# Front half of a hybrid decoder layer: four x tiles and one subtraction for each form, V in four banks, sums read from PSUM, stores spread

## What is computed

```python
h = rms_norm(x, norm_g[l])
proj = jnp.einsum('bsd,de->bse', h, w_in[l])
u_pool, z_pool, q, k, v, z_attn, gate_logits = jnp.split(proj, splits, axis=-1)
y_pool = multiscale_pool(u_pool, pool_w[l], pool_scale[l]) * jax.nn.silu(z_pool)
attn = stick_breaking_attention(q, k, v)
...
x = x + jnp.einsum('bsd,de->bse', merged, w_out[l])
return rms_norm(x, final_g)
```

## Time and profile before

| | |
|---|---|
| median of 3 runs | 1658.92 us (1653.3 to 1668.74) |
| profiled execution | 1660.69 us, of which the span 1658.9 us |
| mean granted clock of TensorE | 0.979 |
| busy PE / DVE / ACT / POOL | 94% / 82% / 50% / 72% of the span |
| front half | up to 439 us of the span |

### The profile page before, as it was taken

The page is one execution under the profiler, slowest core; times in us unless marked ns, Lnnn a source line. Parts: engine busy times, 40 slices in busy tenths (PEclk is TensorE's granted clock), DMA queues, the critical chain, the costliest instruction groups (busy, mean ns, idle before and its releaser), DMA issues. The chain is left out here.

```text
span 1658.9 us, 25189 instructions
## 1 busy us (share of the span) xinstructions
PE 1552.7 (94%) x7770; PEld 1285.2 (77%) x7770; DVE 1354.2 (82%) x1753; ACT 824.9 (50%) x1597; POOL 1188.5 (72%) x818
## 2 busy tenths in 40 slices
PE   7897888988899999899998999999999999999998
PEld 5686666867678788788787788888888878877886
DVE  6987499795699788899789988889988765587988
ACT  4433443332456666566566566666666622133342
POOL 4695585875698877988788788779997534446774
PEclk9998999999999999999999999999999999999999
DMA  6376961247423434334279333343522578764453
GB/s 229 122 276 205 331 196 58 71 121 195 148 84 93 112 100 122 97 100 133 74 231 345 94 106 104 98 119 88 153 78 55 181 241 274 243 219 166 154 190 126
DMA packets 170277, 254.20 MB, mean 153 GB/s; under 512 B 48401, under 2 KB 81681, under 8 KB 170146
## 3 DMA queue, kind: packets, MB, share of 16 engines
q1 hardware_dynamic: 170146, 252.59, 49.5%
HBM read 166.54 MB, written 85.99 MB: 152 GB/s over the span
## 5 line engine op out<-in xcount | busy, mean ns | idle before, releaser
L1828 DVE TENSOR_TENSOR_SCAN left<-keep,left 128x512 f32<-128x512 f32 x192 | 301.3, 1569 | 38.0 <-issue 29.0
L1901 POOL TENSOR_TENSOR ring<-raw,ring 128x512 fp32r<-128x512 f32 x140 | 236.7, 1690 | 80.9 <-ACT ring L1735 65.7
L1655 PE MATMUL psum<-hT,ring 128*128 128x512 f32 x664 | 273.3, 412 | 12.2 <-ACT sum_a L1767 7.0
L1659 PE MATMUL psum<-hT,ring 128*128 128x512 f32 x664 | 271.2, 408 | 0.0
L1657 PE MATMUL psum<-hT,ring 128*128 128x512 f32 x664 | 270.8, 408 | 0.0
L1741 ACT ACTIVATE keep<-psum 128x512 f32<-128x512 f32 (+3 forms) x320 | 171.2, 535 | 128.4 <-PE psum L1678 112.0
L1748 ACT ACTIVATE wt<-psum 128x512 fp32r<-128x512 f32 (+3 forms) x320 | 171.2, 535 | 104.8 <-PE psum L1686 102.1
L1834 DVE TENSOR_TENSOR wt<-psum,wt 128x512 fp32r<-128x512 f32 (+3 forms) x320 | 189.5, 592 | 12.4 <-ACT wt L1748 9.5
L1698 PEld LDWEIGHTS psum<-wt,vm 128*128 128x128 f32 x1088 | 171.4, 189 | 33.9 <-DVE wt L1834 4.3
L1698 PE MATMUL psum<-wt,vm 128*128 128x256 f32 x1088 | 181.8, 282 | 6.4 <-DVE wt L1834 3.5
L1686 PE MATMUL psum<-ident,left 128*128 128x128 f32 x1088 | 171.3, 272 | 11.3 <-DVE wt L1834 11.1
(11 more groups left out here) (240 smaller groups left out, 3597.1 us busy)
## 6 DMA issues: line engine op xcount, KB each, us to landing
raw<-in_w_strips SPq DMA_DIRECT2D x144, 256.0 KB, 4.2
qm<-qk_scratch SPq DMA_DIRECT2D x128, 128.0 KB, 4.2
gate<-gate_scratch SPq DMA_DIRECT2D x64, 256.0 KB, 4.9
form_scratch<-hT SPq DMA_DIRECT2D x28, 512.0 KB, 7.0
hT<-form_scratch SPq DMA_DIRECT2D x28, 512.0 KB, 7.7
xT<-in_x_T SPq DMA_DIRECT2D x16, 512.0 KB, 4.9
qk_scratch<-front_store SPq DMA_DIRECT2D x32, 256.0 KB, 4.3
km<-qk_scratch SPq DMA_DIRECT2D x64, 128.0 KB, 3.8
```

The lines of the kernel that those rows point to most:

```text
L1655: pe.matmul(o, hi, m_hi, start=k == 0, stop=False)
L1659: last = pe.matmul(o, lo, m_hi, start=False, stop=k == HK - 1)
L1828: dve.tensor_tensor_scan(left[:, n % LN, span][:, ::-1], k, k, carry, ALU.mult, ALU.bypass).then_inc(scanned, 1)
L1901: pool.tensor_tensor(out_, a, b, op).then_inc(s, 1)
```

## The change

1. **Forms from x.** T1 to T4 are made from the scaled fp32 tiles, one subtraction each (four for a pair). For that four x tiles are resident; the fourth, `xT_last`, lies in the tile `store`. The load of xT of tile n now waits for T4 of the pair of tile n-4. DVE makes the low of T1 (and T2 of a phase's last pair), POOL the others (before, DVE made three of four, then two of four).
2. **Statistics two tiles ahead**, in the first tile phase: `square`, `mean`, `root`, `factors` of tile n+2 in the step of tile n; the diag is made by ACT. The step of tile 8 comes a slot earlier.
3. **V** has four PSUM banks (two are those of parts 2 and 3), the third product (low with high) of a tile is made in the slot of the next one, `copy_v` three tiles behind, with two staging buffers in turn for V and the mixes.
4. **Sums.** S1 is read from PSUM by DVE, ACT takes A11 only; seven adds per group, no joins. Three output tiles: A12 and A22 share one, S4 has one, S3 has one that lies in `b12`.
5. **Weight forms** S3 and S2 are made by DVE, S1 and S4 stay on POOL.
6. **Stores** of the forms go out three in four slots rather than one in each; V's pieces for stage 3 are asked for after parts 27, 31, 35, 39 rather than 29, 31, 33, 35.

```diff
-ADD_OF = {A12: 1, S2: 2, S3: 3, S4: 4, A22: 5}
+FRONT_ADD = {A12: 1, S2: 2, S1: 3, S3: 4, S4: 6, A22: 7}
+OUT_TILE = {A12: 0, S4: 1, S3: 2, A22: 0}
+OUT_AT = {A12: 1, S3: 5, S4: 6, A22: 7}
+BANK_READ = {A12: 1, S2: 2, S1: 5, S3: 4, S4: 6, A22: 7}
...
+    outs = (out_a, out_b, at("out_c", b12_at, [P, CH], F32)[:, :])
...
+    xT_last = at("xT_last", store_at, [P, KT, P], F32)
...
+    def x_tile(n):
+        return xT[:, n % 4, :, :] if n % 4 < 3 else xT_last[:, :, :]
...
-    V_PARTS = [HALF_PARTS + i for i in (29, 31, 33, 35)]
+    V_PARTS = [HALF_PARTS + i for i in (27, 31, 35, 39)]
...
+    STEP_AT = {n - 1: n for n in range(2, FRONT_TILES)}
+    STEP_AT.update({tile_slot(n) - (2 if n == FRONT_TILES else 1): n for n in range(FRONT_TILES, TT)})
...
-                elif n % FRONT_TILES >= 3:
-                    sp.wait_ge(lo_done, 2 * (n - 2))
-                    if (n - 3) % 2 == 1:
-                        sp.wait_ge(t_raw, RAW_OPS * ((n - 3) // 2) + RAW_OF[T2])
-                sp.dma_start(xT[:, n % 3, :, :], x_T[token_tile(n)]).then_inc(xT_in[n % 3], DMA)
+                    sp.wait_ge(t_raw, 4 * HK)
+                elif n % FRONT_TILES >= 4:
+                    sp.wait_ge(lo_done, 2 * (n - 3))
+                    sp.wait_ge(t_raw, 4 * ((n - 4) // 2 + 1))
+                elif n == FRONT_TILES + 3:
+                    for i in range(2):
+                        sp.wait_ge(hi_stored[i], 4 * qk_before(HALF_GROUPS) // 2 * DMA)
+                sp.dma_start(x_tile(n), x_T[token_tile(n)]).then_inc(xT_in[n % 4], DMA)
...
                 if n is not None:
-                    if n % FRONT_TILES >= 2:
-                        store_v(n - 2)
-                    if n % FRONT_TILES + 3 < FRONT_TILES:
+                    if n % FRONT_TILES >= 4:
+                        store_v(n - 4)
+                    if n % FRONT_TILES + 3 < FRONT_TILES and n != FRONT_TILES:
                         load_xT(n + 3)
                     if n < FRONT_TILES and n + 4 < FRONT_TILES:
...
+                if n == FRONT_TILES + 1:
+                    load_xT(n + 2)
...
-                    if r < len(FORM_LIST):
-                        store_form(*FORM_LIST[r])
+                    for i, form in enumerate(FORM_LIST):
+                        if i * 4 // 3 == r:
+                            store_form(*form)
...
-            def first_forms(n):
-                pair = n // 2
-                if n % FRONT_TILES == 1:
-                    for j in (T2, T1, T3):
+            def first_forms(pair):
+                n = 2 * pair + 1
+                if pair % HK == 0:
+                    for j in (T1, T2):
                         free_home(dve, n, j)
                 dve.wait_ge(scaled_done, 2 * n + 2)
-                dve.wait_ge(lo_done, 2 * n - 1)
+                dve.tensor_tensor(raw_t(n, T1), scaled(n, 0), scaled(n - 1, 0), ALU.subtract).then_inc(t_raw, 1)
+                dve.wait_ge(t_raw, 4 * pair + 1)
+                dve.tensor_tensor(raw_t(n, T2), scaled(n, 1), raw_t(n, T1), ALU.subtract).then_inc(t_raw, 1)
+
+            def last_forms(pair):
+                n = 2 * pair + 1
+                if pair % HK == 0:
+                    for j in (T3, T4):
+                        free_home(dve, n, j)
+                dve.wait_ge(t_raw, 4 * pair + 2)
                 dve.tensor_tensor(raw_t(n, T3), scaled(n, 1), scaled(n, 0), ALU.subtract).then_inc(t_raw, 1)
-                dve.tensor_tensor(raw_t(n, T1), scaled(n, 0), tile_of(n - 1, 0, 0).bitcast(F32),
-                                  ALU.subtract).then_inc(t_raw, 1)
-                dve.wait_ge(t_raw, RAW_OPS * pair + 2)
-                dve.tensor_tensor(raw_t(n, T1), raw_t(n, T1), tile_of(n - 1, 0, 1).bitcast(F32),
-                                  ALU.subtract).then_inc(t_raw, 1)
-                dve.wait_ge(t_raw, RAW_OPS * pair + RAW_OF[T1])
-                dve.tensor_tensor(raw_t(n, T2), scaled(n, 1), raw_t(n, T1), ALU.subtract).then_inc(t_raw, 1)
-
-            def last_form(n):
-                pair = n // 2
-                if n % FRONT_TILES == 1:
-                    free_home(dve, n, T4)
-                dve.wait_ge(t_raw, RAW_OPS * pair + RAW_OF[T2])
-                dve.wait_ge(lo_done, 2 * n)
-                dve.tensor_tensor(raw_t(n, T4), tile_of(n - 1, 1, 0).bitcast(F32), raw_t(n, T2),
-                                  ALU.subtract).then_inc(t_raw, 1)
-                dve.wait_ge(t_raw, RAW_OPS * pair + 5)
-                dve.tensor_tensor(raw_t(n, T4), raw_t(n, T4), tile_of(n - 1, 1, 1).bitcast(F32),
-                                  ALU.add).then_inc(t_raw, 1)
-
...
+                dve.tensor_tensor(raw_t(n, T4), scaled(n - 1, 1), raw_t(n, T2), ALU.subtract).then_inc(t_raw, 1)
+
+            def form_low(pair, j):
+                n = 2 * pair + 1
+                dve.wait_ge(t_hi, 4 * pair + RAW_OF[j])
+                dve.tensor_tensor(low_t(n, j), raw_t(n, j), high_t(n, j).bitcast(F32), ALU.subtract).then_inc(t_lo_dve, 1)
 
             def tile_step(n):
                 i = n % FRONT_TILES
-                first = n < FRONT_TILES
-                if first and i + 1 < FRONT_TILES:
-                    mean(n + 1)
+                first = n < FRONT_TILES and later(n)
+                if first:
+                    mean(n + 2)
                 scale(n)
-                if i + 1 < FRONT_TILES:
-                    if first:
-                        factors(n + 1)
-                    make_diag(n + 1)
+                if first:
+                    factors(n + 2)
                 if i % 2 == 1:
-                    if i >= 3:
-                        form_lows(n - 2)
-                    first_forms(n)
+                    first_forms(n // 2)
                 elif i >= 2:
-                    last_form(n - 1)
+                    last_forms(n // 2 - 1)
+                    form_low(n // 2 - 1, T1)
...
+                value = 7 * g + FRONT_ADD[j]
+                here = bank(FORMS * g + j)
                 if j == A12:
-                    dve.wait_ge(taken, 2 * g + 1)
-                    if not is_u(g):
-                        wait_low_stored(dve, g, A12)
+                    dve.wait_ge(taken, g + 1)
+                    wait_tile_stored(dve, g, A12)
+                    dve.tensor_tensor(out_tile(g, A12), here, sum_a, ALU.add).then_inc(summed, 1)
+                elif j == S2:
+                    dve.tensor_tensor(sum_u, here, sum_a, ALU.add).then_inc(summed, 1)
+                elif j == S1:
+                    dve.wait_ge(summed, value - 1)
+                    wait_tile_stored(dve, g, S4)
+                    dve.tensor_tensor(out_tile(g, S4), here, sum_u, ALU.add).then_inc(summed, 1)
                 elif j == S3:
-                    dve.wait_ge(summed, 5 * g + 2)
-                    wait_low_stored(dve, g, A22)
-                    to = sum_d
+                    dve.tensor_tensor(sum_a, here, sum_u, ALU.add).then_inc(summed, 1)
+                    dve.wait_ge(summed, value)
+                    wait_tile_stored(dve, g, S3)
+                    dve.tensor_tensor(out_tile(g, S3), bank(FORMS * g + S1), sum_a, ALU.add).then_inc(summed, 1)
                 elif j == S4:
-                    dve.wait_ge(joined, 2 * g + 1)
-                    base = sum_e
-                elif j == A22:
-                    dve.wait_ge(summed, 5 * g + 3)
-                    base = sum_d
-                dve.tensor_tensor(to, bank(FORMS * g + j), base, ALU.add).then_inc(summed, 1)
-
-            def join(g, j):
-                if j == S1:
-                    dve.wait_ge(taken, 2 * g + 2)
-                    dve.wait_ge(summed, 5 * g + 2)
-                    wait_low_stored(dve, g, S4)
-                    dve.tensor_tensor(sum_e, sum_a, sum_c, ALU.add).then_inc(joined, 1)
+                    dve.tensor_tensor(out_tile(g, S4), here, out_tile(g, S4), ALU.add).then_inc(summed, 1)
                 else:
-                    dve.wait_ge(summed, 5 * g + 3)
-                    dve.tensor_tensor(out_tile(g, S3), sum_d, sum_c, ALU.add).then_inc(joined, 1)
+                    wait_tile_stored(dve, g, A22)
+                    dve.tensor_tensor(out_tile(g, A22), here, sum_a, ALU.add).then_inc(summed, 1)
...
+            def first_block_forms(g):
+                at_g = blocks[g % 2]
+                dve.wait_ge(block_in[g % 2], (g // 2 + 1) * 4 * DMA)
+                dve.tensor_tensor(at_g[S3][:, :, :], at_g[A11][:, :, :], at_g[S3][:, :, :], ALU.subtract).then_inc(w_first, 1)
+                dve.wait_ge(w_first, 2 * g + 1)
+                if g == 0:
+                    dve.wait_ge(pw_hi_done, 1)
+                    dve.wait_ge(pw_lo_done, 1)
+                else:
+                    dve.wait_ge(w_lo_done, FORMS * (g - 1) + S2 + 1)
+                    dve.wait_ge(w_formed, 2 * g)
+                dve.tensor_tensor(at_g[S2][:, :, :], at_g[A22][:, :, :], at_g[S3][:, :, :], ALU.subtract).then_inc(w_first, 1)
...
             def project_v(n):
```

(43 more changed lines are left out.)

329 lines of the change are left out of this document (174 added, 155 removed).

## The result

The changed kernel takes 1676.55 us (median of 6 runs, 1672.92 to 1680.69) against 1655.95 for the kernel before on the same chip (six runs; the table above has three): ratio 1.0112, 95% interval 1.0078 to 1.0146, which also holds the plain ratio of the medians, 1.0124. It is slower by 1.1%.

What follows compares the result with a forecast made beforehand. It took DVE's pace to hold PE back in the two tile phases. Terms +7, -9, +2 and 0 summed to 0 on the profiled 1660.7 us, less 1.8 to the median: 1659 us, range 1637 to 1681.

Steps and rivals of the forecast that it cites:

- The term for the first tile phase: First tile phase: loads queued behind T4 make DVE wait 6.6 us twice, POOL's chain delays part 2; plus 7 us.
- -3 were the queued loads hidden: First tile phase: without the two 6.6 us waits for queued loads, the phase would come to -3 us.
- Second tile phase: Second tile phase: DVE and POOL work near PE's pace, with one new stall at tile 11; minus 9 us.
- The stall at tile 11: Second tile phase: tile 11's xT load waits for qk stores; DVE idle some 8 us, PE 5.3.
- the forecast end for a covered stall: Second tile phase, best end: -17 us where the stall at tile 11 is covered.
- First part phase: First part phase: cheaper sums against weight forms on DVE and A12 waiting for A22's store; plus 2 us, -6 to +9.
- which shortens landings: First part phase: form stores at three quarters of the rate shorten store landings, set against the A12 wait; no separate size.
- Second part phase: Second part phase: 5 us back from V's later pieces, 5 lost to A12's wait and weight forms; 0, -7 to +8.
- B: Both part phases: A22's store decides, adding +9 and +7 us; whole +22, 1681 us; chance 0.23.
- A: Tile phases: queued loads are covered or short and the relief decides; whole -23, 1636 us; chance 0.25.
- C: V products: "V copy" waits were waits for highs, four banks give nothing; 1663 us; chance 0.52 together with the main forecast.
- the twelve forms: First part phase: twelve weight forms moved from POOL cost DVE 8 to 18 us, mostly hidden.

Runs made afterwards that it cites:

- e1: Changed kernel with each load of x by rows issued ahead of the xT load it stood behind, from tile 5 on; 1668.59 us, ratio 1.0061.
- e9: Changed kernel with e1's load order and V's store of tile n-3 (not n-4) issued in the slot of tile n; 1666.63 us, ratio 1.0042.
- e7: e6 with form stores issued one in each slot, as in the kernel before; 1639.81 us, ratio 0.9865.
- e8: e6 with V's pieces for stage 3 asked for after parts 29, 31, 33, 35 and taken one slot earlier; 1636.74 us, ratio 0.9858.
- e10: e6 with weight forms S3 and S2 back on POOL (e4's edit); 1630.49 us, ratio 0.9824.
- e6: Changed kernel with the edits of e1, e9, e3 and e5, and ACT's wv_hi ahead of tile 1's statistics; 1633.86 us, ratio 0.9844.
- e3: Changed kernel with the xT load of tile 11 issued ahead of tile 12's; 1669.72 us, ratio 1.0074.
- e2: Changed kernel with A12 sharing its output tile with S3 and A22 alone in the other; 1662.19 us, ratio 1.0026.
- e5: Changed kernel with a fourth output tile in b12, for A12; 1658.34 us, ratio 0.9986.
- e4: Changed kernel with weight forms S3 and S2 made by POOL, as in the kernel before; 1679.36 us, ratio 1.0131.

## Why the prediction was right and wrong

**Right in place.** The stalls stood where the order of the queue said. DVE before the mean of tiles 5 and 7: 5.44 and 5.75 us, forecast "some 5". Scale 3 at 41.9 (forecast 39.6, and 2.2 of the difference was lost at the start), scale 7 at 78.4 (74.4), part 2 at 96.1 (93.2). The term for the first tile phase, +7, came out at +8.1 at the first part and, with POOL's chain, at +10.4 at part 2; the 2.3 between them are in the next phase's sum. In the tile phase the queue is worth 6.5 (e1) and V's store behind it 5.5 more (e9 against e1). That store's place was not in the forecast at all, and is the reason why my "-3 were the queued loads hidden" could not be had by e1 alone; with both mended e9 gives -3.9. Nor was the order of `wv_hi` on ACT in the forecast. With it put back, tile 2's first product came at 29.8, 29.7 and 29.7 us in e7, e8 and e10, rather than 31.7: 2 us. In e6 it came at 31.0, but there the first spread itself was 0.9 us late (8.59 against 7.71).

**Second tile phase.** Forecast -9, measured -5.1. Part of the gap is the cut: I counted from the 65.7 us of the earlier trace rows, and against those 58.5 us are -7.2 (and the first part phase is then +20.3). The stall at tile 11 was 8.2 us on DVE (forecast some 8) and 7.8 on PE (forecast 5.3). e3 takes 7.0 us off the phase; the forecast end for a covered stall (-17) would be 48.7, e3 and e6 give 51.4 and 53.0.

**First part phase: the step that failed.** Forecast +2 ("PE feels it only beyond three slots"), measured +18.3; the end that I gave for it was +9. The mechanism was named, A12 behind A22's store, but sized wrongly in three ways. I put DVE's wait at 3 to 5 us, twice, from landings of 6.0 and 7.4 less one slot of 2.7. The trace shows 5.5 to 8.0, three times in this phase, because A22's store is not issued a slot behind its sum: its high first waits for a store of its own (5.91 us), so 9.1 us pass. I then priced only the bank that PE waits for. What stands behind A12's high on ACT I named but gave no price: the mix scale (a PE stall of 7.75 us, 2.76 in e2), and the diag of tile 8 (6.14 us), which the change had moved to ACT and which I left out. And the slower products behind these stalls cost 6.3 us, part of the same loss. The spread form stores that I set against all this, "which shortens landings", show no such gain: the high stores landed in 6.5 us in e6 and in 5.2 in e7, where they are not spread. e2 and e5 put the price of the sharing at 15.8 and 20.0 us.

**Second part phase.** Forecast 0, measured -1.8. DVE's wait at L123 fell from 10.4 to 8.3 us only, yet PE's 5.0 went; e8, where the pieces are back in their old places and the phase is 1.4 us longer, shows that these places matter little. The sharing cost 4.7 us here (e5). The loss is smaller than in the first phase, where DMA had a share of 0.71 against 0.49 here; that this is the reason is not shown. The phase also has the wait at its end: PE's first product of stage 3 waited 7.0 us before and 3.7 after, where I had put 0.

**The rivals.** B (slower, 1681) is what happened by its mechanism. Its time came near in part by luck: it had +9 and +7 for the two part phases, where +18.3 and -1.8 came, and stages 3 and 4 gave 4.8 us that nobody forecast. The range holds the measured time only because it reached to B's centre. B had 0.23 and should have had the larger part, since the loop could be read from the order: store, high, low, store, sum. A did not come; e6 shows that its premise, the relief, was there to be had: with the loads and the stores out of the way the kernel takes 1633.9, near A's 1636, though by other terms (A had nothing for the part phases, and the fourth output tile took 20 and 4.7 us off those of the changed kernel). C's reading of the waits fits the trace, where waits for highs and diags took the place of those for V's copy; no run has two banks again, so what four banks and the deferred products are worth is not shown. Nor is it shown which part of the change gives the 1.6% of e6: three of its parts, undone in e7, e8 and e10, can't be told from nothing; the forms from x, the statistics ahead and the sums from PSUM were not undone.

**The weight forms.** I gave the twelve forms 8 to 18 us of DVE, mostly hidden (at the 1.8 us each that I named as the most, twelve are 21.6). e4 takes them off again: DVE's busy time in the phase falls by 8.5 us (108.2 to 99.7), and the phase doesn't move, so none of it shows on the path of the changed kernel.

The Trainium skill, "SBUF — State Buffer", section on the two sides, has DVE and GpSimd hold their shared port pair under an exclusive lock, each for a whole instruction; by that rule alone the move frees as much as it takes. e4 and e10 don't speak against it, as far as their intervals can tell.

**Sums that don't come out.** Two more figures in the working are off by little. The arrival of tile 11's high adds up to 245.1 us, not 245.5. And "47 with POOL's pace" is 18.7 below 65.7, not 17. Neither moves the forecast by more than 2 us.

## What to carry to other kernels

When two results share a buffer, take the time from the first result's sum to the landing of its store along every wait in between, and set it against the time until the second result's sum; then list all that stands behind the waiting instruction on each engine. In a queue issued in order, put loads that wait for late results behind those that don't, also when both were harmless before. When several parts are changed at once, a real gain can hide behind stalls that can be mended one by one: here stalls of 42.6 us stood over a gain of 1.6%.

## What was not expected of the hardware

The operation that the change added to the statistics (L999, two inputs of 128x1) takes 0.16 us alone and up to 1.18 us while POOL works, with a median of 0.76 over the 16 tiles. The one at 45.37 above took 1.13 us and ended at 46.50, as POOL's operation did (46.47):

```profile
45.20 1.27 POOL L747 TENSOR_TENSOR hT<-xT_last,hT 128x512 fp32r<-128x512 f32 x1
```

L997 with one input, just ahead of it, stays at 0.15. So its price was up to 1.2 us a tile, not the 0.2 that I gave it: here a small operation with two SBUF inputs waited beside POOL as a large one did. Form stores issued one in each slot did not lengthen the landing of the high stores (5.2 against 6.5 us, one trace each, above).
